# mLSTM values with the weights stationary and v moving, tokens on partitions, as three single-pass products of rounded parts and remainders

## What is computed

```python
def step(carry, inp):
    C, n, m = carry
    ...
    a = jnp.einsum('bhtd,bhsd->bhts', qc, kc) * w_loc
    num = w_st[..., None] * jnp.einsum('bhvd,bhtd->bhtv', C, qc) + jnp.einsum('bhts,bhsv->bhtv', a, vc)
    den = w_st * jnp.einsum('bhd,bhtd->bht', n, qc) + a.sum(axis=-1)
    h = num / jnp.maximum(jnp.abs(den), jnp.exp(-m_t))[..., None]
    ...
for direction in range(2):
    ...
    h_lat = h_lat + flip(hl)
return (h.transpose(0, 2, 1, 3).reshape(o.shape) * o).astype(o.dtype)   # o = sigmoid of the output gate
```

## Time and profile before

| | us |
|---|---|
| median of 3 runs | 2641.15 |
| lowest and highest | 2636.52, 2644.75 |
| profiled execution | 2640.15 |
| its span, first to last instruction | 2638.5 |
| TensorE busy | 2555.6 (97%) |
| VectorE busy | 1588.3 (60%) |
| ScalarE busy | 934.7 (35%) |
| GpSimd busy | 210.8 (8%) |

### The profile page before, as it was taken

One profiled execution on the slowest core, in us unless ns is written; L12 is line 12 of the kernel. 1 busy time (PEld: TensorE's weight loads), 2 busy tenths in 40 slices (PEclk: granted clock), 3 DMA queues, 4 the chain that ended last, 5 costly groups with the idle time before them and its releaser, 6 DMA issues.

```text
span 2638.5 us, 39421 instructions
## 1 busy us (share of the span) xinstructions
PE 2555.6 (97%) x15252; PEld 2173.2 (82%) x15252; DVE 1588.3 (60%) x1822; ACT 934.7 (35%) x1235; POOL 210.8 (8%) x264
## 2 busy tenths in 40 slices
PE   4999999999999998999999999999999999999997
PEld 2788888888646445888899999999999988888886
DVE  5534543474264376336788888888888853333345
ACT  3221212232324324224455555555555542222222
POOL 1000000000106245000000000000000010000000
PEclk8999999999999999999999999999999999999999
DMA  9855555786415543532323223322322362324223
GB/s 352 331 215 215 209 195 194 262 310 217 144 29 125 135 97 116 214 119 100 140 79 137 107 111 125 121 111 108 138 107 111 124 230 98 133 97 142 93 93 108
DMA packets 112360, 402.07 MB, mean 152 GB/s; under 512 B 23696, under 2 KB 41152, under 8 KB 81528
## 3 DMA queue, kind: packets, MB, share of 16 engines
q1 hardware_dynamic: 82608, 295.39, 32.4%
q0 software_dynamic: 15680, 88.28, 8.9%
q10 hardware_dynamic: 14000, 17.44, 1.8%
HBM read 362.81 MB, written 37.47 MB: 152 GB/s over the span
## 4 chain that ended last, share of the span: by engine, by line
PE 56%; DVE 2%; ACT 0%; DMA 0%; issue 0%; POOL 0%; DVEq 0%; ACTq 0%
PE f_ps L2769 25%; PE f_late_ps L2826 13%; PE f_ps L2826 10%; PE f_first_ps L2826 7%; DVE h L2735 0%; PE f_late_ps L2793 0%; PE f_ps L2780 0%; DVE x_lo L2587 0%; DVE f_lo L2491 0%; DVE h L2581 0%; PE f_first_ps L2845 0%; DVE f_lo L2411 0%; DVE f_c L2536 0%; DMA f_raw<-in_w_up 0%; DMA f_u_raw<-u_spill 0%
## 5 line engine op out<-in xcount | busy, mean ns | idle before, releaser
L2769 PE MATMUL f_ps<-f_u_hi,f_hi 128*128 128x512 f32 x671 | 262.6, 391 | 1.4 <-DVE f_lo L2411 1.4
L2769 PE MATMUL f_ps<-f_u_hi,f_lo 128*128 128x512 f32 x671 | 262.6, 391 | 0.0
L2769 PE MATMUL f_ps<-f_u_lo,f_hi 128*128 128x512 f32 x671 | 262.5, 391 | 0.0
L2514 DVE SCALAR_TENSOR_TENSOR h<-f_ps,mod,h 128x512 f32<-128x512 f32 (+1 forms) x76 | 57.1, 751 | 316.4 <-PE f_ps L2769 316.4
L619 PE MATMUL i_ps<-hn_hi,i_hi 128*128 128x512 f32 x608 | 240.5, 395 | 0.0
L619 PE MATMUL i_ps<-hn_hi,i_lo 128*128 128x512 f32 x608 | 239.7, 394 | 0.0
L619 PE MATMUL i_ps<-hn_lo,i_hi 128*128 128x512 f32 x608 | 238.5, 392 | 0.0
L2165 ACT ACTIVATE f_hi<-f_raw 128x1408 fp32r<-128x1408 f32 (+1 forms) x82 | 123.1, 1501 | 294.6 <-PE f_ps L2769 275.9
L2491 DVE TENSOR_TENSOR f_lo<-f_s,f_hi 128x1024 fp32r<-128x1024 f32 x160 | 195.6, 1222 | 42.5 <-ACT f_hi L2195 42.5
L493 DVE TENSOR_TENSOR i_lo<-i_raw,i_hi 128x2048 fp32r<-128x2048 f32 x38 | 87.0, 2291 | 218.3 <-ACT i_hi L357 218.3
L2195 ACT ACTIVATE f_hi<-f_s 128x1024 fp32r<-128x1024 f32 x160 | 168.7, 1055 | 81.6 <-PE f_late_ps L2826 36.4
(11 more groups left out here) (419 smaller groups left out, 6735.7 us busy)
## 6 DMA issues: line engine op xcount, KB each, us to landing
f_raw<-in_w_up SPq DMA_DIRECT2D x88, 1024.0 KB, 5.1
i_ring<-in_ada_rest POOLq DMA_DIRECT2D x64, 1024.0 KB, 5.3
f_raw<-in_w_down SPq DMA_DIRECT2D x64, 704.0 KB, 4.1
i_raw<-in_w_in SPq DMA_DIRECT2D x38, 1024.0 KB, 4.9
i_ring<-in_ada_first SPq DMA_DIRECT2D x32, 1024.0 KB, 7.3
f_raw<-in_w_out SPq DMA_DIRECT2D x16, 1024.0 KB, 4.8
u_spill<-f_u SPq DMA_DIRECT2D x44, 256.0 KB, 2.1
f_u_raw<-u_spill POOLq DMA_DIRECT2D x44, 256.0 KB, 4.7
```

Of the source, the lines that this page charges most:

```text
L2514: nc.vector.scalar_tensor_tensor(ht, pt[s][:, :], mod[:, bass.ds(group * KT + m, 1), 0:1].rearrange("p a b -> p (a b)"), ht, ALU.mult, ALU ...
L2769: mm = nc.tensor.matmul(pt[s][:, :], m[:, k, :], v(k, slice(0, SEQ)), start=(k == 0 and n == 0), stop=(k == len(ks) - 1 and n == 2))
```

## The change

Values are computed the other way round, and in three single-pass products.

- The weighted products of a slot are split: `high(n)` on ScalarE copies them rounded to fp32r into one of two tiles `ring_hi`, `low(n)` on VectorE writes the remainder, in place, as fp32r. v is split the same way, once per head (`values_high` on ScalarE, `values_low` on VectorE; for head 0 inside `one`, for the others in steps i = 2 and i = 3 of the head before). `v_hi` of the last three heads lies in space of `one`.
- `values(n)`: for each direction and each block of 128 queries, the block of weighted products is stationary and v (192 columns and 2 of ones) moves: high x high, high x low, low x high. A context tile has 8 blocks and 24 matmuls, a latent one 5 blocks and 15. The results have queries on partitions, two blocks per PSUM bank; the denominators are column 192.
- Head's end: `inverse` (VectorE, three operations on 8 columns) with floors that now come as columns of `ccol` (four more transposes in `stage_mla`; `em`, its two stores and its load are gone), `scaled` (ScalarE, four blocks of direction 1), `summed` (VectorE, four blocks of direction 0 plus the former), `turn` (TensorE, eight transposes), `gated` (VectorE, two). `floors`, `invert`, `spread`, `turn_floors`, `invert_columns`, and POOL's `added` and `gated` are gone. POOL keeps the masks; its memset of ones goes to the stage's start.
- Scores have two PSUM banks instead of three. The order of weights(n+3), loads and masks stays; in ScalarE's order high(n) stands behind weights(n+3), in VectorE's order products(n+1) stands ahead of low(n).

```diff
-                sp.wait_ge(em_ok, 2)
-                for d in range(2):
-                    sp.dma_start(em[4 * d:4 * d + 4, :], emr[32 * d:32 * d + 4, :]).then_inc(rows_st, 16)
...
+                        pe.wait_ge(em_ok, 2)
+                        for t in range(QT):
+                            mm = nc.tensor.transpose(c_ps[:, (KEYT + t) * 36:(KEYT + t + 1) * 36], emr[:, t * P:(t + 1) * P],
+                                                     ident[0:36, 0:36])
...
-                sp.wait_ge(rows_st, 64)
+                sp.wait_ge(rows_st, 32)
...
-                two.load_floors(sp)
...
-                    if u == 1:
-                        two.turn_floors(pe)
-                    if u in (2, 3):
-                        two.spread(pe, ML_H - 1, u - 2)
+                    if u == 2:
+                        two.turn(pe, ML_H - 1)
 
                 def ready(u):
                     if u == 0:
                         pe.wait_ge(na_ld, 16 * 3)
                     if u == 2:
-                        pe.wait_ge(two.oe_ok, 4 * ML_H)
-                three.tensor(pe, after, ready, lambda: pe.wait_ge(two.h_ok, 4 * ML_H), lambda: pe.wait_ge(nv_ld, 16 * (4 * QT + 1)))
+                        pe.wait_ge(two.hs_ok, QT * ML_H)
+                three.tensor(pe, after, ready, lambda: pe.wait_ge(two.hg_ok, 2 * ML_H), lambda: pe.wait_ge(nv_ld, 16 * (4 * QT + 1)))
...
+                def values_high():
+                    act.wait_ge(ml_ld, 16 * (2 + KEYT))
+                    two.values_high(act, 0)
+                one.scalar(act, head_out, drain, values_high)
...
+            if u == UNITS - 4:
+                aside()
...
+            if u == UNITS - 5:
+                aside()
...
+    ring_hi = [arena.at(f"g_ring_high{n}", [P, 1024], NSM_AT + 4096 * n, F32R) for n in range(2)]
...
+    s_ps = [banks[:, n, :] for n in range(2)]
+    b_ps = [banks[0:HALF, n, :] for n in (2, 7)]
+    HALF_BANK = SEQ // 2
+
+    def acc(d, t):
+
+        at = HALF_BANK * (t % 2)
+        return banks[:, 3 + 2 * d + t // 2, at:at + ML_VW]
+
+    def den_sums():
+
+        return banks[:, 3:7, :].rearrange("p b (j c) -> p (b j) c", c=HALF_BANK)[:, :, ML_D:ML_D + 1].rearrange(
+            "p (d t) c -> p d (t c)", d=2)
+
+    def blocks(st, d):
+
+        if st >= QT:
+            return [(t, t + QT * (1 - d)) for t in range(QT)]
+        return [(t, t) for t in range(st + 1)] if d else [(t, t + 1) for t in range(st, QT)]
...
+    def values_high(act, h):
+
+        act.wait_ge(z_ok, 1)
+        nc.scalar.activation(v_hi[h][:, :, :], v[:, :, h, :], ACT.Copy).then_inc(vh_ok, 1)
+
+    def values_low(dve, h):
+
+        dve.wait_ge(vh_ok, h + 1)
+        nc.vector.tensor_tensor(v_lo[:, :, h, :], v[:, :, h, :], v_hi[h][:, :, :].bitcast(F32), ALU.subtract).then_inc(vl_ok, 1)
+
+    def columns(n):
+
+        return 2 * SEQ if ORDER[n % KEYT] >= QT else SEQ + P
+
+    def high(act, n):
+
+        s, w = n % SLOTS, columns(n)
+        act.wait_ge(a_ok, products_done(n))
+        if n >= 2:
+            act.wait_ge(v_ok, n - 1)
+        nc.scalar.activation(ring_hi[n % 2][:, 0:w], ring[s][:, 0:w], ACT.Copy).then_inc(ah_ok, 1)
+
+    def low(dve, n):
+
+        s, w = n % SLOTS, columns(n)
+        dve.wait_ge(ah_ok, n + 1)
+        nc.vector.tensor_tensor(ring_lo[s][:, 0:w], ring[s][:, 0:w], ring_hi[n % 2][:, 0:w].bitcast(F32), ALU.subtract).then_inc(al_ok, 1)
+
     def scalar(act):
-        def read_sums(h):
-            act.wait_ge(v_ok, KEYT * (h + 1))
+        def scaled(h):
+            act.wait_ge(d_ok, 3 * (h + 1))
             if h >= 1:
-                act.wait_ge(ha_ok, 2 * h)
-            for d in range(2):
-                for n in range(2):
-                    nc.scalar.activation(num[:, 2 * d + n, :], o_ps[d][n], ACT.Copy).then_inc(oe_ok, 1)
+                act.wait_ge(hs_ok, QT * h)
+            for t in range(QT):
+                nc.scalar.activation(part[:, t, :], acc(1, t)[:, 0:ML_D], ACT.Copy, scale=den[:, 1, t:t + 1]).then_inc(pt_ok, 1)
 
         weights(act, AHEAD - 1)
         for n in range(UNITS):
             if n + AHEAD < UNITS:
                 weights(act, n + AHEAD)
-            if n % KEYT == KEYT - 1:
-                read_sums(n // KEYT)
-
-    def floors(dve, h):
+            high(act, n)
+            if n % KEYT == 2 and n // KEYT + 1 < ML_H:
+                values_high(act, n // KEYT + 1)
+            if n >= KEYT and n % KEYT == 0:
+                scaled(n // KEYT - 1)
+        scaled(ML_H - 1)
...
+    def inverse(dve, h):
+
+        floor = ccol[:, KEYT:KEYT + QT, h:h + 33:32].rearrange("p t d -> p d t")
+        dve.wait_ge(v_ok, KEYT * (h + 1))
+        if h >= 1:
+            dve.wait_ge(pt_ok, QT * h)
+        nc.vector.scalar_tensor_tensor(den[:, :, :], den_sums(), -1.0, floor, ALU.mult, ALU.max).then_inc(d_ok, 1)
+        dve.wait_ge(d_ok, 3 * h + 1)
+        nc.vector.tensor_tensor(den[:, :, :], den[:, :, :], den_sums(), ALU.max).then_inc(d_ok, 1)
+        dve.wait_ge(d_ok, 3 * h + 2)
+        nc.vector.reciprocal(den[:, :, :], den[:, :, :]).then_inc(d_ok, 1)
+
+    def summed(dve, h):
+
+        dve.wait_ge(d_ok, 3 * (h + 1))
+        if h >= 2:
+            dve.wait_ge(tu_ok, 2 * (h - 1))
+        for t in range(QT):
+            dve.wait_ge(pt_ok, QT * h + t + 1)
+            nc.vector.scalar_tensor_tensor(hs[h % 2][:, t, :], acc(0, t)[:, 0:ML_D], den[:, 0, t:t + 1], part[:, t, :], ALU.mult,
+                                           ALU.add).then_inc(hs_ok, 1)
+
+    def gated(dve, h):
 
         if h == 0:
+            dve.wait_ge(ml["og_ld"], 16)
+        if h >= 2:
+            dve.wait_ge(stored, 16 * (h - 1))
+        for a in range(2):
+            dve.wait_ge(tu_ok, 2 * h + a + 1)
+            nc.vector.tensor_tensor(ho[h % 2][:, a, :], b_ps[a], og[:, 2 * h + a, :], ALU.mult).then_inc(hg_ok, 1)
...
+        products(0)
         for n in range(UNITS):
-            products(n)
+            if n + 1 < UNITS:
+                products(n + 1)
+            low(dve, n)
             h, i = n // KEYT - 1, n % KEYT
+            if i == 3 and h + 2 < ML_H:
+                values_low(dve, h + 2)
             if h >= 0:
                 if i == 0:
-                    floors(dve, h)
-                elif i < 3:
-                    invert(dve, h, i - 1)
-                elif i < 5:
-                    scaled(dve, h, i - 3)
+                    inverse(dve, h)
+                    summed(dve, h)
+                elif i == 2:
+                    gated(dve, h)
+        inverse(dve, ML_H - 1)
...
+            summed(dve, ML_H - 1)
...
+    def turn(pe, h):
+
+        pe.wait_ge(hs_ok, QT * (h + 1))
+        for a in range(2):
+            if h >= 1:
+                pe.wait_ge(hg_ok, 2 * (h - 1) + a + 1)
             for t in range(QT):
+                mm = nc.tensor.transpose(b_ps[a][:, t * P:(t + 1) * P], hs[h % 2][:, t, a * HALF:(a + 1) * HALF], ident[:, :])
+            mm.then_inc(tu_ok, 1)
 
...
-            pe.wait_ge(a_ok, products_done(n))
-            for d in range(2):
-                for a in range(2):
-                    if i == 0 and h >= 1:
-                        pe.wait_ge(oe_ok, 4 * (h - 1) + 2 * d + a + 1)
-                    if st >= QT:
-                        to, frm = slice(0, SEQ), slice(SEQ * (1 - d), SEQ * (2 - d))
-                    else:
-                        w1, w0 = lat_widths(st)
-                        to, frm = (slice(st * P, SEQ), slice(w1, w1 + w0)) if d == 0 else (slice(0, w1), slice(0, w1))
-                    mm = nc.tensor.matmul(o_ps[d][a][:, to], v[:, st, 2 * h + a, :], ring[s][:, frm], start=(i == 0),
-                                          stop=(i == KEYT - 1), skip_group_check=True)
+            pe.wait_ge(al_ok, n + 1)
+            if i == 0:
+                pe.wait_ge(vl_ok, h + 1)
+            for d in (1, 0):
+                for t, at in blocks(st, d):
+                    if i == 0 and h >= 1 and t % 2 == 0:
+                        pe.wait_ge(pt_ok if d else hs_ok, QT * (h - 1) + t + 2)
+                    mine = slice(at * P, (at + 1) * P)
+                    for m, (w, x) in enumerate(((ring_hi[n % 2], v_hi[h][:, st, :]), (ring_hi[n % 2], v_lo[:, st, h, :]),
+                                                (ring_lo[s], v_hi[h][:, st, :]))):
+                        mm = nc.tensor.matmul(acc(d, t), w[:, mine], x, start=(i == 0 and t % 2 == 0 and m == 0),
+                                              stop=(i == KEYT - 1 and m == 2), skip_group_check=True)
             mm.then_inc(v_ok, 1)
 
         for n in range(UNITS):
             if n + 2 < UNITS:
                 score(pe, n + 2)
-            if n == 0:
-                pe.wait_ge(z_ok, 1)
             values(n)
-            if n == KEYT:
-                pe.wait_ge(z_ok, 2)
-                pe.wait_ge(c_ld, 32)
-            h, i = n // KEYT - 1, n % KEYT
-            if h >= 0 and i in (2, 3):
-                spread(pe, h, i - 2)
-
```

(5 more changed lines are left out.)

173 lines of the change are left out of this document (50 added, 123 removed).

## The result

The changed kernel takes 2646.62 us (median of 17 runs, 2641.25 to 2654.41), the kernel before 2641.51 us (17 runs beside it, 2636.27 to 2645.70): ratio 1.0022, 95% interval [1.0012, 1.0032]. The difference is small, 5.1 us, but the interval leaves out 1: the changed kernel is slower, by 0.1 to 0.3%, and the forecast took 0.3% for the least that can be told. The time lies within the range, 2.6 us above the number forecast. The runs of the changed kernel go with the mean granted clock that each lists: 2641.25 us at 0.993, 2653.48 and 2654.41 at 0.985. The profiled execution is the one of 2641.25 us, the fastest; the profiled one of before took 2640.15.

What follows compares the result with a forecast made beforehand. The mLSTM loop, bound by TensorE, was to become bound by the refill chain. -3.1 + 0.3 + 0.4 + 10.7 - 7.3 + 2.0 = +3.0 us on 2640.15 gives 2643.2, 2644 for the median; range 2630 to 2662.

Steps and rivals of the forecast that it cites:

- the refill chain: mLSTM loop: values(n) queue behind a row refill that starts when values(n-2) end; 30.6 us per middle head.
- Rival 2: mLSTM loop: the ring chain hides and TensorE stays the bound; kernel at 2617 to 2622 us; chance 0.10.
- Rival 3: mLSTM loop: refills get longer, 12 us in all per microsecond; 2656 us at 1 us more; chance 0.20.
- Rival 4: mLSTM values: a narrow product takes four passes, 0.323 us; kernel near 2711 us; chance 0.08.
- The price of a product: mLSTM values: a narrow single-pass product takes 0.116 us, next to the weight-load rate; ends 0.094 and 0.120.
- Rival 1: mLSTM values: the weight load hides and a narrow product costs 0.094 us; kernel at 2639 us; chance 0.12.
- The clock: mLSTM loop: idle stretches lower TensorE's clock in two or three dips, 2 us added, bounds 0 and 5.
- The heads: mLSTM loop: 30.6 us per middle head; heads 2, 3 and 4 start at 927.7, 958.3 and 988.9.
- the sign of being right: mLSTM loop: periods of 29 to 31 us in heads 2 and 3, TensorE 75 to 80% busy there.
- The barrier: In front of stage_heads: comes 3.1 us earlier, as SP no longer issues the two em transfers.
- Behind the loop: From the loop's end into the next stage: 7.3 us back, the sixth turn 18.2 us behind the loop.
- the sum: Whole kernel: all terms together, +3.0 us on the profiled execution's 2640.15, so 2643.2 us.

Runs made afterwards that it cites:

- e1: The changed kernel with ScalarE's rounding of unit n issued ahead of the exponentials of unit n+3; 2627.75 us.
- e7b: The changed kernel with a small useless load, waited for by SP, ahead of each refill of a row slot; 2681.91 us.
- e10: e1 with two more swaps at the head boundary: inverse ahead of the remainder, scaled parts ahead of the exponentials; 2617.07 us.
- e12: e10 with the next stage's loads issued one at a time over units 6 to 17, wide slabs first; 2612.52 us.
- e5: The changed kernel with the second and third product of each block on 128 of the 194 moving columns; 2668.66 us.
- e4: The changed kernel with four useless 512-column matmuls (three in the first head) ahead of each head's first values; 2641.30 us.
- e2: The changed kernel with the stores of the em rows put back on SP ahead of the wait for R; 2651.64 us.
- e6: The changed kernel without the product of the rounded weights and v's remainder, two products per block instead of three; 2635.03 us.
- e11: e10 with a useless load ahead of each refill of a row slot; 2647.73 us.

## Why the prediction was right, and where it wasn't

- *The mechanism.* Shown, by e1, e7b and the timeline: the refill chain bounds the loop up to the last head, not TensorE. Rival 2 (the chain hides) fell. Its 2617 to 2622 us is what e10 gives once the queue's order is mended, but partly by luck: its loop was 88.8 us (894.2 to 983.0), and e10's is 101.5 and e12's 92.6. Rival 3 (longer refills) was right in its mechanism and near in its price: it said 12 us for each microsecond of a longer refill, and in e7b 3.6 us on average cost the loop 39.3, 11 for each. But in the changed kernel the refills stayed at what I had taken (issue to mask 3.7 us for the one of 940.18, against 3.9), except in the first head (4.6 to 5.0 us for those of 905.61, 910.95 and 915.69). Rival 4 fell: the product is one pass.
- *The price of a product.* 0.112 us against 0.116 forecast, and not set by the moving columns (e5); that the load sets it is what is left, and fits the 0.113 us of loads with one moving column. Rival 1's 0.094 is not reached as a mean in any run. Nor is the sustained 0.081 us that the Trainium skill gives for a load and a matmul ("TensorE: Matmul & The Clock Gate", section "Back-to-back issue gap"). But the 0.162 us that I gave 194 columns at 1.2 GHz was wrong: at the lower level the products come every 0.213 us, twice 0.107. What bounds the product slows with the clock too. The 0.107 us that the Trainium skill has for the load (same page, section "LDWEIGHTS") fits the full clock only.
- *The clock.* This is the term that was mis-sized. I had 2.0 us with bounds 0 and 5; the loop took 121.8 us where chain and products gave 114.1, 7.7 more. The last head shows it by itself: 21.9 us at a clock of 0.84, 18.6 us at full clock in e12 (959.03 to 977.67), 19.4 in the forecast. Filling the boundaries alone got 5.3 us back (e4). I had counted "two or three such dips"; there were five. The mistake was to price dips one by one, when the new loop makes an idle boundary in every head. The Trainium skill, "TensorE: Matmul & The Clock Gate", section "HAM oscillation — how this bites in real kernels", describes a loop that waits for a transfer each time round and starts each round at the lower clock. Here the wait is for the accumulators, once per head, and the trace agrees, with a stretch at the lower level behind each of the four boundaries.
- *The heads.* 32.9 and 31.8 us against 30.6, just outside the 29 to 31 that I had named as the sign of being right; the first 35.3 against 33.5. The last is in the point above. TensorE was busy for 84 and 82% of the middle heads, not 75 to 80, since its products took longer at the lower clock. The clock makes the difference: a head's first 24 products at 0.213 instead of 0.112 us are 2.4 us (unit 6, unit 18), and by the mean distance of the products in each unit the five slow ones cost 2.4, 2.4, 1.5, 1.6 and 0.8 us, 8.7 in all. Without them the heads are 32.9, 30.5, 30.3 and 19.5 us, where the forecast had 33.5, 30.6, 30.6 and 19.4.
- *The barrier.* -3.1 us, as forecast. *Forgotten:* the 2.0 us of lower clock in before's first softmax units, that went with its idle of 4.8 us. It stood in the trace of before.
- *Behind the loop.* -8.5 against -7.3; the next stage's first turn is at 1013.80, 6.3 us behind the loop (forecast 6 to 7), the sixth at 1025.99, 18.5 us behind it (forecast 18.2).
- *How the errors met.* Clock in the loop +5.7 more than forecast, clock at the softmax loop -2.0, finish -1.2, the start of the program -3.2 by the clock that the two executions happened to meet there, the rest -1.2: the profiled execution came out 1.9 us under the sum. The median lies 5.4 us above that execution, which had the highest clock of all, 0.993 where the run at the median had 0.990. So the cost of the clock was probably larger in most runs than in the one that was profiled; where, no trace shows. The forecast was close, but partly by terms that cancelled.

## What to carry to other kernels

When a step is put between two engines, look at which *queue* it goes into and what stands in front of it there: here one swapped line on ScalarE was worth 19 us, where the whole change moved 5. Look for the same thing at each boundary and in the queue that feeds the loop. And when a change moves the bound from TensorE to a chain, price the clock with the chain: here each idle stretch at a boundary was paid again in what followed it, at 0.213 instead of 0.112 us per product.

## What the hardware showed that I had not expected

- The clock can stay at its lower level while TensorE works without a pause: 61.4 us in e5, with 0.213 us per product and 128 or 194 moving columns. With 194 columns in all products the longest such stretch without a wait was 6.8 us in the changed kernel, 10.2 in e2 and 13.7 in e6.
- These products take 0.112 us at full clock and 0.213 us at the lower level, whether all three of a block have 194 moving columns or two of them 128.
- A load of 64 KB that took 2.8 to 3.2 us in front of most of e7b's refills took 6.1 us there, and 6.2 in e11, when SP had issued two wide slabs ahead of it.
